# Key lookups of a routed expert layer on GpSimd, and eight dense panels moved to later batches

## The reference, cut to what matters

```
q  = (xn @ w_query) in 8 heads of 256                 # 2048 pairs of token and head
s1, s2 = q[:128] . sub_keys_1, q[128:] . sub_keys_2   # 128 scores each
v1,i1 = top16(s1);  v2,i2 = top16(s2)
top, pos = top16 of the 256 sums v1[a] + v2[b]
expert = 128 * i1[pos >> 4] + i2[pos & 15]            # one of 16384
gate   = softmax(top)
hidden = gelu(xn . expert_u[expert]) * gate
out   += hidden * expert_v[expert]                    # a row of 2048 numbers each
```

## Time and profile before

| what | value |
|---|---|
| median of 3 runs | 2957.23 us (2957.08 to 2959.57) |
| the profiled execution's own time | 2961.6 us |
| its span in the profile | 2959.4 us |
| busy: PE / DVE / ACT / POOL | 93% / 64% / 44% / 22% |
| read from HBM | 944.95 MB |
| moved by DMA | 790.37 MB, mean 267 GB/s |

### The profile page before, as it was taken

How to read it: one execution, slowest core, us unless ns; L and a number is a source line. 1 busy time by engine, 2 the same in 40 slices (tenths; PEclk the granted TensorE clock), 3 DMA queues, 4 the chain that set the end, 5 groups by cost and what they waited for, 6 DMA issues and landing times.

```text
span 2959.4 us, 47035 instructions
## 1 busy us (share of the span) xinstructions
PE 2748.9 (93%) x18175; PEld 2078.1 (70%) x18175; DVE 1881.6 (64%) x3067; ACT 1296.6 (44%) x2473; POOL 663.6 (22%) x576
## 2 busy tenths in 40 slices
PE   8999899999999998999999999999998878888885
PEld 8996788888888887989999889677764432222221
DVE  7885566565565565455445558888858874555556
ACT  5555443333333344435334345555566532233223
POOL 0000000000000000040000002444447675555554
PEclk9999999999999998999999999999996679999997
DMA  6443545555555553443555656999999999999998
GB/s 257 176 166 127 199 174 189 192 184 185 189 193 184 186 190 124 157 147 141 183 185 184 241 199 243 372 408 417 412 385 411 405 407 423 422 422 419 419 419 347
DMA packets 132598, 790.37 MB, mean 267 GB/s; under 512 B 34774, under 2 KB 34774, under 8 KB 37142
## 3 DMA queue, kind: packets, MB, share of 16 engines
q1 hardware_dynamic: 55040, 393.16, 35.9%
q0 software_dynamic: 77008, 394.46, 33.0%
q10 hardware_dynamic: 384, 0.52, 0.1%
HBM read 944.95 MB, written 4.19 MB: 321 GB/s over the span
## 4 chain that ended last, share of the span: by engine, by line
PE 65%; DMA 17%; DVE 10%; issue 4%; ACT 2%; POOL 2%; POOLq 0%; DVEq 0%; ACTq 0%
PE bank L2073 12%; PE bank L2074 12%; PE bank L2075 12%; DMA s_u<-in_expert_u,s_u_index 11%; PE bank L2079 10%; PE bank L2515 5%; DMA s_v<-in_expert_v,s_v_index 5%; PE bank L2080 5%; DVE s_u L1933 3%; PE bank L2570 3%; PE bank L2525 2%; DVE s_w_lo L1306 1%; POOL s_u L658 1%; DVE s_yrow L1614 1%; PE bank L2171 1%
## 5 line engine op out<-in xcount | busy, mean ns | idle before, releaser
L1306 DVE TENSOR_TENSOR s_w_lo<-s_raw,s_w_hi 128x2048 fp32r<-128x2048 f32 x288 | 661.3, 2296 | 597.0 <-ACT s_w_hi L705 592.9
L705 ACT ACTIVATE s_w_hi<-s_raw 128x2048 fp32r<-128x2048 f32 x284 | 543.9, 1915 | 805.6 <-PE bank L2075 530.0
L2079 PE MATMUL bank<-s_a,s_w_hi 128*128 128x512 f32 x1408 | 495.0, 394 | 3.2 <-DVE s_w_lo L1306 3.2
L2073 PE MATMUL bank<-s_a,s_w_hi 128*128 128x256 f32 (+1 forms) x1632 | 465.5, 285 | 3.4 <-DVE s_a L1330 1.8
L2075 PE MATMUL bank<-s_a,s_w_lo 128*128 128x256 f32 (+1 forms) x1632 | 463.1, 284 | 0.0
L2074 PE MATMUL bank<-s_a,s_w_hi 128*128 128x256 f32 (+1 forms) x1632 | 462.7, 284 | 0.0
L1933 DVE CUSTOM_DVE_ANT_0 s_u<-s_u,s_xn_late 128x1024 f32<-128x1024 f32 x256 | 304.0, 1225 | 223.7 <-DMA s_u<-in_expert_u,s_u_index 197.3
L2570 PE MATMUL bank<-s_v,s_spread 128*32 128x512 f32 x2048 | 309.0, 715 | 139.3 <-DMA s_v<-in_expert_v,s_v_index 107.0
L2080 PE MATMUL bank<-s_a,s_w_lo 128*128 128x256 f32 x1408 | 395.3, 281 | 0.0
L658 POOL DMA_INDIRECT s_u<-in_expert_u,s_u_index x256 | 297.4, 1162 | 359.9 <-DVE s_halfdot L1933 207.3
L678 POOL DMA_INDIRECT s_v<-in_expert_v,s_v_index x256 | 311.5, 1217 | 231.0 <-PE bank L2570 140.3
(11 more groups left out here) (352 smaller groups left out, 3397.4 us busy)
## 6 DMA issues: line engine op xcount, KB each, us to landing
s_raw<-in_stream SPq DMA_DIRECT2D x292, 1024.0 KB, 4.8
s_raw<-in_expert_v SPq DMA_DIRECT2D x40, 1024.0 KB
s_raw<-in_dense_u SPq DMA_DIRECT2D x37, 1024.0 KB
s_tap_blocks<-in_taps POOLq DMA_DIRECT2D x9, 512.0 KB, 3.5
s_u<-in_expert_u,s_u_index POOLq DMA_INDIRECT x256
s_v<-in_expert_v,s_v_index POOLq DMA_INDIRECT x256
s_panel_early<-in_dense_u POOLq DMA_DIRECT2D x3, 1024.0 KB, 10.8
s_xres<-in_x SPq DMA_DIRECT2D x2, 1024.0 KB, 6.0
```

The lines of the kernel that those rows point to most:

```text
L705: act.activation(w_hi[s % 2][:, :], raw[s][:, :], ACT.Copy).then_inc(hi_ready, 1)
L1306: dve.tensor_tensor(w_lo[s % 2][:, :], raw[s][:, :], w_hi[s % 2][:, :].bitcast(f32), ALU.subtract)\
L2073: pe.matmul(dst, left[0], right[0], start=start, stop=False)
L2079: pe.matmul(dst, left[0], both, start=start, stop=False)
```

## The change

1. `u_panels_in`: steps 0 to 15 compute two panels each (0 to 31), steps 16 to 23 one each (32 to 39).
2. The comparison, product and sum of the pair lookup leave DVE for POOL, for the 13 heads routed within the batches. DVE computes the positions in the third turn instead of the fourth and signals `pos_ready`. POOL runs `pairs_picked_of(th)` behind the gathers with k = 4g + 8, where g is the batch that routed the head; DVE waits for `pairs_picked` in the third turn of batch g + 1 and makes experts and indices there. ACT makes the second table's indices a batch later. The key numbers of two heads are kept (`ind` twice).
3. Panels 32 to 39 are multiplied into the upper half of bank 4 or 5. ACT applies gelu in place in PSUM. Their eight rows of `ha` hold 1.0 from a memset on POOL at k = 48, take the gates with `gated` like the others, and are multiplied by the gelu in `late_panel` on DVE, in the second turn of the batch two after the panel's step. A panel from the third of them on waits for `late_panel` of the one two before.
4. What waited for 40 panels now waits for 32: the transposed gates, the banks. The waits for all 40 (`xn_late`, and the panels of the second table) stay.

```diff
+FIRST_DENSE = 32
 def u_panels_in(i):
-    if i == 0:
-        return range(2)
-    if i == 17:
-        return range(DENSE - 1, DENSE)
-    return range(2 + 37 * (i - 1) // 16, 2 + 37 * i // 16) if i < 17 else range(0)
+    if i < 16:
+        return range(2 * i, 2 * i + 2)
+    return range(i + 16, i + 17) if i < 16 + DENSE - FIRST_DENSE else range(0)
...
+            def pairs_picked_of(th):
+
+                both = pool_pick[:, :].rearrange("p (s a) -> p s a", a=TOPK)
+                halves = pool_pick[:, :].rearrange("p (h k a) -> p h k a", h=2, a=TOPK)
+                pool.wait_ge(pos_ready, th - EARLY + 1)
+                step(pool.tensor_copy(pool_ind[:, :], ind[th % 2][:, :]))
+                link(pool.tensor_copy(pool_pos[:, :], pos_of[:, :]))
+                link(pool.tensor_tensor(both, iota_f[:, 0:TOPK].unsqueeze(1).to_broadcast([128, 2 * TOPK, TOPK]),
+                                        pool_pos[:, :].unsqueeze(2).to_broadcast([128, 2 * TOPK, TOPK]), ALU.subtract))
+                link(pool.tensor_scalar(both, both, 0.0, None, ALU.is_equal))
+                link(pool.tensor_tensor(halves, halves, pool_ind[:, :].rearrange("p (h a) -> p h a", h=2).unsqueeze(2).to_broadcast([128, 2, TOPK, TOPK]),
+                                        ALU.mult))
+                for width in (8, 4, 2):
+                    link(pool.tensor_tensor(both[:, :, 0:width], both[:, :, 0:width], both[:, :, width:2 * width], ALU.add))
...
+                pool.tensor_tensor(keys_of, halves[:, :, :, 0], halves[:, :, :, 1], ALU.add).then_inc(pairs_picked, 1)
...
+                if k == 12 * BATCH:
+                    pool.wait_ge(expert_ready, PH)
+                    pool.memset(ha[:, 0:DENSE - FIRST_DENSE, :], 1.0).then_inc(late_cleared, 1)
+                if k % BATCH == 0 and k >= 2 * BATCH and route_in(k // BATCH - 2):
+                    pairs_picked_of(route_in(k // BATCH - 2))
...
+                if d >= FIRST_DENSE:
+                    half = bank[4 + d % 2][:, T:2 * T]
+                    act.activation(half, half, ACT.Gelu_apprx_tanh).then_inc(late_gelu, 1)
+                    return
...
+            def late_panel(d):
+
+                dve.wait_ge(late_gelu, d - FIRST_DENSE + 1)
+                dve.wait_ge(late_cleared, 1)
+                row = ha[:, dense_block(d), :]
+                dve.tensor_tensor(row, row, bank[4 + d % 2][:, T:2 * T], ALU.mult).then_inc(late_gated, 1)
+                dve.wait_ge(late_gated, d - FIRST_DENSE + 1)
...
                     if turn == 2 and g and route_in(g - 1):
+                        dve.wait_ge(pairs_picked, route_in(g - 1) - EARLY + 1)
+                        experts_of(route_in(g - 1))
                         gates_softmax(route_in(g - 1))
...
+                if d < FIRST_DENSE:
+                    into(b, d // 4)
+                elif d < FIRST_DENSE + 2:
+                    into(b, FIRST_DENSE // 4)
+                else:
+                    pe.wait_ge(late_gated, d - FIRST_DENSE - 1)
+                dst = bank[b][:, 0:T] if d < FIRST_DENSE else bank[b][:, T:2 * T]
```

More of the change, by code:

```diff
@@ L403, in two_layers @@
     one_key = place("s_one_key", [128, 16 * NKEYS], S + 16 * K)
-    one_key_more = small("s_one_key_more", 8 * NKEYS)
+    more_at = spot(8 * NKEYS)
+    one_key_more = place("s_one_key_more", [128, 8 * NKEYS], more_at)
+    pool_pick = place("s_pool_pick", [128, 2 * TOPK * TOPK], more_at)
+    pool_pos = place("s_pool_pos", [128, 2 * TOPK], more_at + 8 * TOPK * TOPK + 128)
+    pool_ind = place("s_pool_ind", [128, 2 * TOPK], more_at + 8 * TOPK * TOPK + 256)
     pick_at = spot(2 * TOPK * TOPK)
@@ L413, in two_layers @@
     val = small("s_val", 2 * TOPK)
-    ind = small("s_ind", 2 * TOPK, u32)
+    ind = [small("s_ind0", 2 * TOPK, u32), place("s_ind1", [128, 2 * TOPK], more_at + 8 * TOPK * TOPK, u32)]
     top = small("s_top", TOPK)
@@ L488, in two_layers @@
         expert_ready, v_index_ready = sem("expert_ready"), sem("v_index_ready")
+        late_cleared, late_gelu, late_gated = sem("late_cleared"), sem("late_gelu"), sem("late_gated")
+        pos_ready, pairs_picked = sem("pos_ready"), sem("pairs_picked")
         gate_max, gate_exp = sem("gate_max"), sem("gate_exp")
@@ L1243, in one_keys @@
                 act.activation(four, four, ACT.Relu, scale=-1.0, bias=1.0).then_inc(one_key_ready, 1)
-            slots_stored = [n.after(f"empty{6 + t}", DENSE // 4 + 1) for t in range(TT)]
+            slots_stored = [n.after(f"empty{6 + t}", FIRST_DENSE // 4 + 1) for t in range(TT)]
             for g in range(ROUTES * GROUPS):
@@ L1262, in _ @@
                         gate_exps(route_in(g - 1))
-                        v_indices(route_in(g - 1))
+                    if g > 1 and route_in(g - 2):
+                        v_indices(route_in(g - 2))
                     for d in u_panels_in(g - 1):
@@ L1896, in pairs_experts @@
                                        pos_of[:, :].unsqueeze(2).to_broadcast([128, 2 * TOPK, TOPK]), ALU.is_equal))
-                link(dve.tensor_tensor(halves, halves, ind[:, :].rearrange("p (h a) -> p h a", h=2).unsqueeze(2).to_broadcast([128, 2, TOPK, TOPK]),
+                link(dve.tensor_tensor(halves, halves, ind[th % 2][:, :].rearrange("p (h a) -> p h a", h=2).unsqueeze(2).to_broadcast([128, 2, TOPK, TOPK]),
                                        ALU.mult))
@@ L1919, in route @@
                     best_pairs()
-                else:
-                    pairs_experts(th)
+                    step(dve.tensor_scalar(pos_of[:, 0:TOPK], pos[:, :], 4, None, ALU.logical_shift_right))
+                    dve.tensor_scalar(pos_of[:, TOPK:], pos[:, :], TOPK - 1, None, ALU.bitwise_and).then_inc(pos_ready, 1)
             def dot(k):
@@ L1951, in one_keys_2 @@
                     for t in range(TT):
-                        dve.wait_ge(bank_empty[6 + t], n.after(f"empty{6 + t}", DENSE // 4 + 1))
+                        dve.wait_ge(bank_empty[6 + t], n.after(f"empty{6 + t}", FIRST_DENSE // 4 + 1))
                 wait(dve, one_key_used, 2 * (m - 2))
@@ L1964, in gated @@
                 if group == 0:
+                    dve.wait_ge(late_cleared, 1)
                     for a in range(2):
-                        dve.wait_ge(bank_empty[4 + a], n.after(f"empty{4 + a}", DENSE // 4))
+                        dve.wait_ge(bank_empty[4 + a], n.after(f"empty{4 + a}", FIRST_DENSE // 4))
                 dve.wait_ge(one_key_used, GATE_TOKENS // 4 * (group + 1))
@@ L2037, in _ @@
                         route(route_in(g), turn)
+                    if turn == 1 and g > 16:
+                        for d in u_panels_in(g - 2):
+                            if d >= FIRST_DENSE:
+                                late_panel(d)
                     fours = token_fours_in(g)
@@ L2503, in dense_u_panel @@
             def dense_u_panel(d):
-                b = 4 + (d + 2) % 4
+                b = 4 + (d + 2) % 4 if d < FIRST_DENSE else 4 + d % 2
                 if d == 0:
                     pe.wait_ge(xnt_ready, 1)
-                into(b, d // 4)
+                if d < FIRST_DENSE:
[5 more added lines that the diff above has]
+                dst = bank[b][:, 0:T] if d < FIRST_DENSE else bank[b][:, T:2 * T]
                 if d < NE:
@@ L2533, in slots_transposed @@
                 pe.wait_ge(gates_ready, PH * (t + 1))
-                into(6 + t, DENSE // 4)
+                into(6 + t, FIRST_DENSE // 4)
                 for kind in range(3):
@@ L2542, in token_four @@
                 if f % 2 == 0:
-                    into(b, DENSE // 4 + 1 + f // 4)
+                    into(b, FIRST_DENSE // 4 + 1 + f // 4)
                 pe.wait_ge(one_key_ready, f + 1)
@@ L2556, in blocks_turned @@
                 if g < TURNED[2]:
-                    into(4 + g % 2, DENSE // 4)
+                    into(4 + g % 2, FIRST_DENSE // 4)
                 pe.wait_ge(diagonal_ready, g - TURNED[0] + 1)
@@ L2585, in _ @@
                     for b in (4, 5):
-                        into(b, DENSE // 4)
+                        into(b, FIRST_DENSE // 4)
                     for b in (6, 7):
-                        into(b, DENSE // 4 + 1 + T // GATE_TOKENS // 2)
+                        into(b, FIRST_DENSE // 4 + 1 + T // GATE_TOKENS // 2)
                     pe.wait_ge(xres_back, 16)
+                    pe.wait_ge(late_gated, DENSE - FIRST_DENSE)
                     residual(1)
```

15 lines of the change are left out of this document (10 added, 5 removed).

## The result

| what | before | after |
|---|---|---|
| median of the runs on the same chip (4 each) | 2957.4 us (2957.08 to 2959.57) | 2982.52 us (2979.77 to 2983.76) |
| the profiled execution's own time | 2961.6 us | 2981.88 us |
| its span | 2959.4 us | 2980.0 us |

The ratio is 1.0079, 95% interval 1.0067 to 1.0091: slower by 25 us in the medians and by 20.6 in the spans. The 4.4 us between them are those by which the profiled execution of before lies above its median. Forecast were 2965, so 8 slower, and 2942 to 2984. The sign and the range held; the size was wrong by 17 us, and the time lies outside what the forecast case alone allowed (2957 to 2975).

The account below looks back on a forecast made before the run. DVE, PE and DMA were taken to bound routed batches within 0.8 us of each other, under DMA's 422 GB/s. Stages summed 0 - 7 - 5 + 13 + 10 = +11, bytes gave +8, taken: 2965 us, range 2942 to 2984.

Parts of the forecast that it names:

- forecast case: Main forecast for the whole kernel: 8 us slower, 2965 us, alone allowing 2957 to 2975; chance 0.42.
- B: Batches 14 to 16: with fewer panels on PE, 49 us instead of 56.2; term -7, bounds -9 and 0.
- C: Batches 17 to 19: hole behind step 16's three panels closes, 58.5 us instead of 63.3; term -5, bounds -8 and +8.
- The ceiling and the holes: From about 1850 us on: DMA's ceiling 422 GB/s; window shortfalls in time, the holes, total 31 us, the most gainable.
- The forecast from the bytes: Cross-check by DMA shortfall from batch 1 on: 39 us of holes instead of 31, so +8, taken as the forecast.
- A: Batches 1 to 13, lookup on POOL: blocking eats DVE's saved 2.18 us, period stays about 20.5; term 0, bounds -19 to +18.
- D: Batches 20 to 23: a panel each makes them 17.5 us instead of 14.2; term +13, bounds +9 and +45.
- E: Batches 24 and 25: postponed loads of 4 MB fall among gathers; term +10, bounds +5 and +10.
- The lookup is nearly free: Rival, batches 1 to 13: DVE loses only 0.5 us, batches run at DMA's 18.9; 2949 us; chance 0.25.
- POOL becomes the bound: Rival, batches 1 to 13: late gathers, 22 us per routed batch, +18 us, 2983 us; chance 0.13.
- PE falls to 1.2 GHz: Rival, steps 18 to 23: half clock, half of the batches at 24 us; +25, 2990 us; chance 0.07.
- The holes merely move: Rival, whole kernel: DMA carries the same bytes, nothing measurable, within 6 us of 2957; chance 0.13.

Follow-up runs that it names:

- e3: Full change, but in steps 18 to 23 PE's late panel stands behind the token fours and ACT's gelu behind the copies; 2969.94 us, 1.004 against before.
- e2: Full change with the whole lookup back on DVE, so only the eight late panels move; 2975.11 us, 1.0059 against the kernel before.
- e1: Kernel before with only the lookup moved to POOL, the 40 panels staying in steps 0 to 17; 2965.35 us, 1.0025 against before.
- e4: Kernel before, its lookup kept on DVE, with the same operations added on POOL on constants, result unused; 2980.09 us, 1.0073 against before.
- e10: e8 with the whole lookup on POOL; 2967.5 us, 1.0032 against the kernel before.
- e8: e7 with 36 panels in steps 0 to 15 and only four late ones, in steps 16 to 19; 2957.61 us, 0.9996 against the kernel before.
- e7: e2 with the order of e3: all eight late panels behind the fours, lookup on DVE; 2961.68 us, 1.0013 against the kernel before.

## Why the prediction was right or wrong

**Why the range held: by luck.** The forecast case alone ran to 2975. The upper end of the range, 2984, was there for POOL as the bound at 22 us per routed batch, and that did not happen: routed batches took 20.3 on average. What filled it was mostly the order on PE, felt in batches 19 and 20, 13 of the 25 us, for which no term and no rival stood. The steps that failed are named under B and C.

**The ceiling and the holes: right, and the way to the size.** The stretch can be no faster than its bytes at 422 GB/s, and the change was to be judged by holes. Forecast were 39 us of holes; e3, the change in the better order, has 39.5, the change 51.5. The forecast from the bytes held for batches 1 to 13 (23.5, measured 24.0), though for another reason: it put all 10 us to four panels fewer, and these alone made 5.0 (e2 has 18.5), the lookup 5.5. It failed for 14 to 19 (3, measured 10.3) and 20 to 23 (4, measured 10.5). 24 to 61 were put at 8.5 and came to 6.6.

**A, batches 1 to 13: 0, measured +0.3, in other parts than said.** DVE lost the three operations of 2.18 us as put. The blocking was put at 2.2 and measured 1.1 (11.8 us in 11 lookups). POOL's own operations were put at 6.3 with 2.5 of waiting; the means of the nine in this window sum to 8.7 (for example 1.97 for the comparison, 1.32 for the product), so this was right. The step "all of that goes", of POOL's idle time, was right in the main: POOL's idle behind dot products fell from 81.1 to 12.6 us in these batches. What I left out is that a full POOL gives late gathers: the waits for picked keys and rows (9.7 and 7.1) made up for the smaller blocking. Nor did I see that the bytes DMA misses by it (383 GB/s) fall due later.

The Trainium skill, SBUF — State Buffer, section "SBUF: two separate sides", says that of DVE with two SBUF inputs and POOL whichever starts first keeps the shared ports for its whole instruction. The five half dot products that began within POOL's product in batches 1 to 13 agree: they took 2.17 to 2.31 us instead of 1.22. One of them, in POOL's timeline of after, behind a comparison:

```profile
2071.40 1.50 POOL L697 TENSOR_SCALAR s_pool_pick<-s_pool_pick 128x512 f32<-128x512 f32 x1
2072.99 1.44 POOL L698 TENSOR_TENSOR s_pool_pick<-s_pool_pick,s_pool_ind 128x512 f32<-128x512 f32 x1
```

and DVE's:

```profile
2072.07 1.23 DVE L1974 CUSTOM_DVE_ANT_0 s_u<-s_u,s_xn 128x1024 f32<-128x1024 f32 x1
...
2073.22 2.29 DVE L1974 CUSTOM_DVE_ANT_0 s_u<-s_u,s_xn 128x1024 f32<-128x1024 f32 x1
```

The second half dot product began 0.23 us into the product and took 2.29 instead of 1.22, so it waited 1.07 of the 1.21 that were left. A comparison with one operand does otherwise: the first half dot product began with 0.83 us of it left and lost nothing. Another meeting, on POOL:

```profile
2026.46 2.35 POOL L697 TENSOR_SCALAR s_pool_pick<-s_pool_pick 128x512 f32<-128x512 f32 x1
```

and DVE:

```profile
2026.13 1.32 DVE L1974 CUSTOM_DVE_ANT_0 s_u<-s_u,s_xn 128x1024 f32<-128x1024 f32 x1
...
2027.38 1.62 DVE L1974 CUSTOM_DVE_ANT_0 s_u<-s_u,s_xn 128x1024 f32<-128x1024 f32 x1
```

The comparison takes 1.50 at 2071.40 and 2.35 here, so it did wait, by about what the first half dot product still had to go; the second began within the comparison, which ran for another 1.43 us, and lost only 0.40. So the 13 us that the prediction gave for the page's rule on top did not come: by these rows the rule holds for POOL's two-operand product, and overprices the comparison, the longest of the nine. Here the measurement decides.

**B, batches 14 to 16: -7, measured 0.** The failed step is "12.8 for 14, about 16 for 16". It is near for panels alone: e2 has -10.4. But I counted the lookup in batches 1 to 13 only, as if it ended with them, and I priced these batches without what was owed. POOL works at the lookup a batch later, in batches 14 and 16 too, which are short and need a gather pair each 3.2 us. They took 15.8 and 20.4; the same holds for batch 7 (16.4 for 12.8). And DMA was near its limit: 22.8 MB at 406 GB/s. My own figures for three batches and five panels give 3 x 5.88 + 5 x 1.05 = 22.9 MB, 54 us at 422; a forecast of 49 needed batches 1 to 13 to bring more than their share, as they do in e2, and with the lookup they did not. How much of the 7 us is late gathers in these batches is not separated; the hole in them is 2.1 us, before had 1.1. Together with e1 (+9.2 by the end of batch 16) and e2 (-9.1), this closes: the full change stands at +0.3 there.

**C, batches 17 to 19: -5, measured -0.2.** The failed step is "0.3 + 1.5 + 5.3 + 7.1 + 4 x 1.98 = 22, or 21": it adds PE's work and takes it for the batch. PE's work was right (23.1 busy in batch 19), but the order in which it stands made DVE wait 8.3 us ahead of its dot products, and the batch took 25.1. Batch 20, of the next term, lost in the same way. Batch 17 was put at 16.5 and took 19.4, with DMA at 423 GB/s: it moved 8.2 MB where my sum has 6.9, owed bytes again. With the panel behind the fours the term is 55.7 - 63.3 = -7.6, in its bounds.

**D, batches 20 to 23: +13, measured +14.6, right in sum for a wrong reason.** By PE's work I had 17.5 four times. The batches took 21.3, 15.8, 17.2 and 17.2. In e3's order they take 63.5 in all, +6.7: below my lower bound of +9, which took DMA's mean for a limit in each batch, while 17 to 19 had already moved some of the bytes ahead (in e3 22.8 MB, where three batches with a panel each are 20.8; 20 to 23 then moved 25.3 instead of 27.7). So 8 us of the 14.6 are the order and the rest is the panels. The upper bound, +45, does not follow from the 28 us a batch given for it, which make +55; nothing rested on it.

**E, +10, measured +5.3** in batches 24 and 25 of the full change, and 37.0 - 28.3 = +8.7 in e3. In both DMA is the limit (412 and 417 GB/s). The two batches moved 3.9 MB more than before in e3, as put, but 2.3 MB more in the full change, whose loads were all issued in batch 24, from 2299.4 us on. So fewer gathers came in beside them; why stays open.

**The rivals.** "The lookup is nearly free" fell by e1, e4 and e10. "POOL becomes the bound" is in part what happened: not with a period of 22 but in short batches and late gathers, 7.4 us instead of 18. "PE falls to 1.2 GHz" fell: the granted clock in batches 20 to 23 is 0.92, and was 0.69. The Trainium skill, TensorE: Matmul & The Clock Gate, section "What's actually happening", has sustained work release the clock; the trace agrees. "The holes merely move" is what e8 shows with half as many panels moved; in the change itself they grew by 20 us.

**What my list of signs was worth.** Half dot products above 1.22 with some over 2, batches 1 to 13 at "about 385" (383), a routed batch at 20 to 21 us (20.3 on average), DVE's three operations gone: all seen. POOL's idle before u gathers fell from 97.3 to 29.5 us, of which each gather's own 0.3 is a large part. Of its operations of 512 numbers only the comparison was often at 2 us or more. "17 to 19 above 400" was not seen (367), and that was the sign of the step that failed. Nor was "17 to 18 us each" for 20 to 23: they took 21.3, 15.8, 17.2 and 17.2, and 15.8 is below the 16.5 that I had named as proof against me. What is still open: e1's span is 3 us better than its holes say, and e10's too; how much of the order's 13 us is ACT's order or the lower clock; and whether a lookup split in several pieces between gathers would cost less.

## What to carry to other kernels

When work is moved between batches, add up each engine's work, but then write down the order on the engine and ask who waits for what stands behind the moved piece: panels of 7 us, one in each of six steps, cost 13 us more ahead of the last fours (4 us of work) than behind them, where all eight late panels together cost 3.3 (e7). On the engine that issues the gathers, idle time is not free to be filled: its slack is what lets short batches catch up. Count a full queue there as late gathers, and their missing bytes as owed in the batches after the moved work. And where a kernel runs near the rate of its DMA, measure every version by its holes: they show which lead will last and which will be given back. They don't show the cause; for that it took one change at a time.
